# Shifted copies of a gated chunk: one DMA of whole rows in place of four DMAs of short pieces

## The reference

```python
def conformer_conv_module(h, w_pw1, b_pw1, w_dw, b_dw, ln_g, ln_b, w_pw2, b_pw2):
    a, g = jnp.split(h @ w_pw1 + b_pw1, 2, axis=-1)
    u = a * jax.nn.sigmoid(g)
    u = causal_depthwise_conv(u, w_dw) + b_dw        # 31 taps, channel by channel
    u = jax.nn.silu(layer_norm(u, ln_g, ln_b))
    return u @ w_pw2 + b_pw2
```

## Time and profile before

| | |
|---|---|
| median of 3 runs | 2377.85 us (2376.82 to 2378.49) |
| profiled execution, whole | 2377.77 us |
| its span, first to last instruction | 2375.9 us |
| TensorE busy | 2315.3 us, 97% |
| VectorE busy | 1330.1 us, 56% |
| ScalarE busy | 874.9 us, 37% |
| mean granted TensorE clock | 0.994 of 2.4 GHz |

### The profile page before, as it was taken

How to read it: one execution, slowest core, us unless ns; L and a number is a source line. 1 busy time by engine, 2 the same in 40 slices (tenths; PEclk the granted TensorE clock), 3 DMA queues, 4 the chain that set the end, 5 groups by cost and what they waited for, 6 DMA issues and landing times.

```text
span 2375.9 us, 36384 instructions
## 1 busy us (share of the span) xinstructions
PE 2315.3 (97%) x14188; PEld 1956.0 (82%) x14188; DVE 1330.1 (56%) x1934; ACT 874.9 (37%) x1337; POOL 3.3 (0%) x5
## 2 busy tenths in 40 slices
PE   9999999999898999999999999999999989999998
PEld 7788888889876888888988877888888777888888
DVE  6564755522667565542366675666633885766523
ACT  6444422222524532222342364333322573333322
POOL 0000000000000000000000000000000000000000
PEclk9999999999999999999999999999999999999999
DMA  4122243332383233333232112333333202333332
GB/s 159 62 63 87 82 125 97 95 93 87 102 181 83 80 106 94 95 96 97 89 104 82 57 60 71 98 97 97 97 97 96 67 28 89 97 97 97 97 90 88
DMA packets 82604, 218.70 MB, mean 92 GB/s; under 512 B 10944, under 2 KB 31808, under 8 KB 82496
## 3 DMA queue, kind: packets, MB, share of 16 engines
q1 hardware_dynamic: 75600, 208.23, 29.1%
q10 hardware_dynamic: 6896, 8.92, 1.3%
HBM read 212.78 MB, written 4.34 MB: 91 GB/s over the span
## 4 chain that ended last, share of the span: by engine, by line
PE 82%; DVE 10%; ACT 5%; issue 2%; DMA 1%; SPq 0%; ACTq 0%; DVEq 0%
PE bank L459 23%; PE bank L461 23%; PE bank L460 23%; PE bank L659 2%; PE bank L658 2%; PE bank L660 2%; DVE w_lo L1603 2%; ACT w_hi L1076 1%; ACT ds L1540 1%; DVE m L1659 1%; DVE acc L1632 1%; DVE h L1664 1%; PE bank L799 1%; DVE small L2255 1%; DVE ds L2274 1%
## 5 line engine op out<-in xcount | busy, mean ns | idle before, releaser
L459 PE MATMUL bank<-u_hi,w_hi 128*128 128x512 f32 (+1 forms) x2090 | 796.8, 381 | 13.7 <-DVE w_lo L1603 6.5
L1076 ACT ACTIVATE w_hi<-raw 128x1024 fp32r<-128x1024 f32 x378 | 399.9, 1059 | 1082.6 <-PE bank L461 944.2
L461 PE MATMUL bank<-u_hi,w_lo 128*128 128x512 f32 (+1 forms) x2090 | 786.8, 376 | 0.0
L460 PE MATMUL bank<-u_lo,w_hi 128*128 128x512 f32 (+1 forms) x2090 | 786.6, 376 | 0.0
L1603 DVE TENSOR_TENSOR w_lo<-raw,w_hi 128x1024 fp32r<-128x1024 f32 x378 | 461.2, 1221 | 400.3 <-ACT w_hi L1076 399.8
L459 PEld LDWEIGHTS bank<-u_hi,w_hi 128*128 128x128 f32 x2090 | 393.3, 188 | 94.2 <-DVE w_lo L1603 7.3
L461 PEld LDWEIGHTS bank<-u_hi,w_lo 128*128 128x128 f32 x2090 | 393.2, 188 | 72.1
L460 PEld LDWEIGHTS bank<-u_lo,w_hi 128*128 128x128 f32 x2090 | 393.6, 188 | 71.2 <-issue 1.2
L459 PE MATMUL bank<-hid_hi,w_hi 128*128 (+1 forms) x440 | 173.4, 394 | 0.0
L461 PE MATMUL bank<-hid_hi,w_lo 128*128 (+1 forms) x440 | 172.5, 392 | 0.0
L460 PE MATMUL bank<-hid_lo,w_hi 128*128 (+1 forms) x440 | 170.8, 388 | 0.0
(11 more groups left out here) (301 smaller groups left out, 2489.3 us busy)
## 6 DMA issues: line engine op xcount, KB each, us to landing
raw<-weights_dram SPq DMA_DIRECT2D x365, 512.0 KB, 3.5
bz<-gated_dram SPq DMA_DIRECT2D x32, 268.0 KB, 5.8
raw<-weights_dram ACTq DMA_DIRECT2D x13, 512.0 KB, 5.1
gated_dram<-bz SPq DMA_DIRECT2D x8, 274.0 KB, 3.3
h<-x_t_dram SPq DMA_DIRECT2D x8, 256.0 KB, 6.0
out_dram<-m SPq DMA_DIRECT2D x4, 256.0 KB, 2.4
out_dram<-m ACTq DMA_DIRECT2D x4, 256.0 KB, 2.5
cmask<-masks_dram ACTq DMA_DIRECT2D x4, 224.0 KB, 4.0
```

Source lines behind the costliest of these rows:

```text
L459: pe.matmul(out, wh, xh, start=start, stop=False)
L460: pe.matmul(out, wh, xl, start=False, stop=False)
L461: return pe.matmul(out, wl, xh, start=False, stop=stop)
L1076: act.activation(w_hi[:, j, :], raw[:, j, :], ACT.Copy).then_inc(hi_ready, 1)
```

## The change

The scratch gets another layout: instead of [group][column] it is the earlier trace rows[group x column], so a row of one chunk has its 16 groups side by side, 16 x 137 columns. A lag is then one shift of the whole row, and `bz4` takes the row as it is, its groups 137 instead of 134 columns apart. The store writes each of the 16 groups' 137 columns to its place in the rows. The four loads, one for each lag, become one whose source is written out as an access pattern over the flat scratch: step 1 for the lag (4 of them), step 2192 for the row (32), and `ROW` = 16 x 137 - 3 = 2189 elements. The destination is all 128 partitions. Each `bz4` buffer now counts 16 for a landing instead of 64. PE's reads keep their expression.

```diff
 LONG = REACH + LAGS - 1
+ROW = GROUPS * LONG - (LAGS - 1)
...
-LANDED = 16 * LAGS
+LANDED = 16
...
-                bz4 = sb("bz4", [P, CONV_RING, GROUPS, REACH], F32, gated)
+                bz4 = sb("bz4", [P, CONV_RING, GROUPS, LONG], F32, gated)
...
-        gated_dram = nc.dram_tensor("gated_dram", (CONV_RING, GROUPS, CHANNELS * PHASES, LONG), F32).ap()
+        gated_dram = nc.dram_tensor("gated_dram", (CONV_RING, CHANNELS * PHASES, GROUPS * LONG), F32).ap()
...
-                sp.dma_start(gated_dram[b].rearrange("g (c r) j -> (g c) r j", r=PHASES), bz[:, c % 2, :, :]).then_inc(bz_kept, 16)
+                kept = gated_dram[b].rearrange("(c r) (g j) -> g c r j", r=PHASES, j=LONG)
+                sp.dma_start(kept, bz[:, c % 2, :, :]).then_inc(bz_kept, 16)
                 sp.wait_ge(bz_kept, 16 * (c + 1))
                 if c >= CONV_RING:
                     sp.wait_ge(conv_full, TILES * (c - CONV_RING + 1))
-                for a in range(LAGS):
-                    of = gated_dram[b].rearrange("g m j -> m g j")[:, :, a:a + REACH]
-                    sp.dma_start(bz4[32 * a:32 * a + 32, b, :, :], of).then_inc(bz4_landed[b], 16)
+                rows = gated_dram[b]
+                shifted = bass.AP(rows.tensor, rows.offset, [[1, LAGS], [GROUPS * LONG, CHANNELS * PHASES], [1, ROW]])
+                to = bz4[:, b, :, :].rearrange("m g j -> m (g j)")[:, 0:ROW]
+                sp.dma_start(to, shifted).then_inc(bz4_landed[b], 16)
```

## The result

The changed kernel takes 2459.55 us (median of 4 runs, 2457.55 to 2461.77), the kernel before 2378.17 us beside it: ratio 1.0338, 95% interval 1.0325 to 1.0351. It is 3.4% slower. The forecast had the direction and the mechanism, but 2407 us, with 2432 us as the upper end; the measured time lies outside.

A forecast was written before the change was run, and what follows sets the result against it. TensorE was taken to be busy nearly everywhere, with two holes in the Conformer stage; four-engine loads would set the pace and delay conv 7 by 29.2 us: 2377.8 + 29.2 = 2407.0 us, range 2384 to 2432 us.

The forecast's parts named there:

- Number of engines: The single shifted load: its source's outermost count of 4 confines it to 4 engines, 32 rows each.
- The schedule: Conformer stage, chunks 0 to 7: stores and loads alternate, mid-stage period 17.4 us against PE's 15.4; conv 7 29.2 us later.
- the last hole: PE's wait before conv 7 at the stage's end: conv 7 moves from 745.15 to 774.4 us, everything behind it too.
- nearly covered: Chunk 1's load: landed at 674.8 us, while PE gets there at about 674, so hardly any wait.
- The rival with hidden loads: Four engines, period 14.2 us under PE's 15.4, so only the stage's ends show: +10 us, 2388 us; chance 0.09.
- the sixteen-engine rival: The load spreads by the destination's 128 rows over 16 engines, 6.3 us gained, 2371.5 us; chance 0.11.
- Price of a row on one engine: The load's 8,756 B rows: 373 ns each from a full queue's rate, 32 rows 11.9 us, bounds 10.9 and 13.8.
- the far bound: The load's 32 rows at the short pieces' rate of 10.7 GB/s: 26 us, not taken because the rows are long.
- Conv 7 ran at half clock already, so nothing is added for it: Last depthwise product: its later start adds no busy time, 0 us, to the forecast.
- The range: Whole kernel: 2384 to 2432 us, leaving out the sixteen-engine cases and the slow rows.
- slow rows on four engines: Rival for the load: 26 us of rows, period 31.5 us, +145 us, 2523 us; chance 0.04.

The follow-up runs named there:

- e2: The changed kernel with the load's source written row outermost, lag inside, partitions of taps and masks renumbered to match: 2379.01 us, ratio 0.9993 to the kernel before.
- f9: The kernel before, short pieces kept, but each lag's load writes every fourth of all 128 partitions, taps and masks renumbered: 2377.75 us, ratio 0.9988.
- f7: e2 with the store of before, 128 pieces of 2,192 B, so the output is not the reference's: 2372.63 us, ratio 0.9976 to the kernel before.

## Why the prediction missed

- **Number of engines: right.** Four, from the tap loads' completions, confirmed by the share of 24% and by e2, where only the order of two dimensions brings 80 us back.
- **The schedule: right in kind.** Store behind load, SP waiting for it, every conv waiting, the last hole the end's. Conv 1, which I had as nearly covered, waited 6.75 us. The rival with hidden loads and the sixteen-engine rival did not occur. (The hidden rival's period is mis-added: 10.9 + 0.8 + 1.5 is 13.2 us, not 14.2; it stays under PE's 15.4 either way.)
- **The step that failed: "Price of a row on one engine".** 373 ns, with 10.9 to 13.8 us as bounds for 32 rows. It measured 544 ns and 17.4 us. The rows I took it from the earlier trace rows are copies over all 128 partitions; e2, which writes those too, has its median row at 331 ns. The price of a byte per engine is not a constant of the engine: it depends on which partitions the others write at the time. At the last load's price this is 8 x 5.5 = 44 us of the 51.4 by which conv 7 (825.78) came later than forecast (774.4). By the packets of all eight loads, with means of 489 to 558 ns a row, it is 41. The rows of the short pieces held the hint: 50 ns for 536 B, half the rate of whole rows. I read it as the cost of short pieces and set its 26 us aside as the far bound; f9 shows that 19 of the 50 ns came from the partitions.
- **The other 10 us.** From first row to last, the eight loads took 156.4 us together, where the forecast had 108.8 (95.2 of rows, 13.6 of weights among them). Beyond the 41 of the rows themselves that is 6 to 7 us of weights and gaps between the rows. All that lies outside these stretches, store and latency, is under 4 us more than forecast, 1.2 of it at the start: SP was let go at 641.96, not 640.8. The store's packets I had too dear: 512 pieces of 36 ns are 1.2 us an engine, not 1.6.
- **"Conv 7 ran at half clock already, so nothing is added for it": right within 0.6 us for conv 7 (5.25 for 4.67 us), and silent on the rest.** With holes of 5 to 17 us all eight products run wholly or partly at half clock, 12 us more busy time. It probably cost little beyond the DMA chain: that chain sets the pace, and with faster products PE would have waited as much longer for the next load. This is argued, no run shows it.
- **The range.** It combined bounds of one kind (rate of whole rows), so that its top, 2432 us, had no case for engines that slow each other. The rival "slow rows on four engines" had such rows, but at 26 us a load and 2523 us; the truth lay between the two.

## What to carry to other kernels

Count a DMA's completions in the trace before its bytes: the outermost dimension of either side, after joining, may confine it to a few engines, and swapping two dimensions of the source decided 80 us here. When a copy runs on few engines, or writes 32 neighbouring partitions, take its price from a row with the same pattern of partitions, not from a whole-tile load. And a layout that makes the load's pieces long makes the store's short: price the whole round, up to the moment at which the waiting engine goes on.

## What was not expected of the hardware

- Two engines moved 128 rows of 8,756 B in 22.1 us, four in 17.5 to 18.0 us, sixteen over all partitions in 4.3 us, sixteen over 32 partitions at a time in 5.8 us.
- A store to DRAM of the same bytes in 512 pieces of 548 B holds its waiter 1.4 to 2.0 us longer than in 128 pieces of 2,192 B where little else is under way (e2 against f7, chunks 0, 4 and 6), though each engine's packets grow by 0.4 us only. Whether it is the length of a piece or its start off any boundary was not separated.
